# The first attention of a three-layer kernel: half of its modulation tiles moved into the output projection, its dense side work spread over two thirds of its units

## The chip, the cores and the metric

The kernel runs on one core of a Trainium2 chip. The core has TensorE (PE, matrix products into PSUM), VectorE (DVE), ScalarE (ACT), GpSimd (POOL) and SyncE (SP); here POOL and SP mostly start DMA transfers. Every engine runs its own instructions in order and waits for others on semaphores. The metric is the device time of one execution in microseconds; three runs were timed and one more was profiled.

## What is computed

The sequence has 512 rows of width 1024. A first block has two layers, a second block one. Each layer of the first block takes six vectors from a conditioning vector c, normalizes x, scales and shifts it, mixes, adds the result times a gate, and does the same with a feed-forward part. The change touches the first layer only, and in it these lines:

```python
cond = jax.nn.silu(c)
mod = cond @ ada_w[i] + ada_b[i]            # six vectors of 1024
sh1, sc1, g1, sh2, sc2, g2 = split(mod, 6)
h = rms_norm(x, norm_mix[i]) * (1.0 + sc1) + sh1
q, k, v = split(h @ w_in, 3)                # 16 heads of 64, q and k normalized
s = q k^T + bias                            # block-causal: the future is cut off
y = (softmax(s) v) @ w_out
x = x + g1 * y
h = rms_norm(x, norm_ffn[i]) * (1.0 + sc2) + sh2
x = x + g2 * (square(relu(h @ w1)) @ w2)
```

The gate g1 is needed when y is added, sc2 and sh2 when x is normalized right behind it, and g2 only at the end of the feed-forward part.

## The kernel before

**Dense products.** Weights come as 136 slabs of 128 x 2048. SP loads a slab into one of two `w_raw` buffers; ACT rounds it into `w_hi` (line 1022); DVE subtracts to get `w_lo` (line 1444, `split`). The activations are kept as such a pair too (`h_hi`, `h_lo`), and each product is three matmuls (`three`, line 472): high by high, high by low, low by high. Splits run one slab ahead of PE: slab n + 1 is split at the start of the step in which PE uses slab n. PSUM has eight banks; an engine that has emptied a bank says so in `acc_free`.

**Modulation tiles.** `mod` is not computed on PE. POOL loads one tile of 128 x 1024 of `ada_w` (512 KB) at a time (line 396) into one of two `ada_raw` buffers, and a single DVE instruction multiplies it with c and sums along the row (line 1472, `ada`); the result is one column of `mod`, 128 of its values. A tile's transfer is issued when the tile two before it has been used (`ada_used`). `ada_put` (line 1482) adds the offsets. In the first layer tiles 0 to 31 are used up to the end of the projections, tiles 32 to 39 are sc2, 40 to 47 are g2.

**The attention.** It is written out as steps s, one for each unit s of 64. A unit is one head and one block `it` of 128 query rows; with `it` from 0 to 3 the score width n grows from 128 to 512 columns, and eight units (four blocks of two heads) make a head pair. In step s:
- PE (`attention_a`, line 635 on) makes the scores of units s and s + 1 if s is even (line 643), the transposes of unit s - 4 (line 652), and for even s the products with v of units s - 6 and s - 5 (line 666), then calls `side`.
- DVE (line 1858 on) adds the bias and takes the row maximum of unit s (line 1869), splits a slab where the plan says so, and for odd s scales units s - 3 and s - 2 by the inverse row sums (lines 1878, 1880). Where s is 6 more than a multiple of 8 it takes the finished output of a head pair out of PSUM. At every fourth step from 8 to 68 it does one `ada` at the end of the step.
- ACT (line 1155 on) first does the slab's high part if the plan says so and copies a side unit's result (line 1145), then copies the transposes of unit s - 4 (line 1165) and takes the exponential of unit s (line 1171).

**The side work.** v of the last eight heads is not computed ahead. It is left as eight side units of 24 matmuls (`pair_a`: one block of rows times 256 columns) from two slabs, 10 and 11, four units each. The plan `SIDE_A` lists the steps at which PE does them; slab 11 is split at the first step listed, slab 12 at the fifth. `value_a` makes PE wait for all eight before head 8. Since the side units read `h_hi` and `h_lo`, into which the attention's outputs are to go, the outputs of the first three head pairs are kept in `a_oT` (`A_EARLY`), and turned into their high and low parts at the steps of `A_KEPT`.

**The output projection.** `tail` multiplies with slabs 12 to 15. PE takes slabs 12 and 13 whole (outputs 0 to 3 of eight), then slabs 14 and 15 for the first half of the columns, then both again for the second half. On DVE and ACT the order is: split slab 13, outputs 0 and 1, split slab 14, outputs 2 and 3, split slab 15, outputs 4 to 7 by halves. DVE adds an output to x (line 1523, halves line 1510), ACT squares it (line 1076), DVE accumulates the squares (line 1505); the sums are the next normalization's. `tail` takes a function that is called behind each of the first three splits; before the change none is given here.

Of the kernel before, what the change touches and what calls it, by code (L numbers as in the profile page):

```python
# [15 lines left out]
TT = T // P  # L16
# [29 lines left out]
ADA_TILES = 48  # L46
# [4 lines left out]
ADA_QKV = 16  # L51
# [2 lines left out]


A_HEADS, HD = 16, 64
A_EARLY = 3

SG_HALF, SG_GROUPS = 3072, 8

# [14 lines left out]
def program(nc, I, out, tab_d, tz_d):  # L75
    ctx = ExitStack()
    with ctx:
        sems = {}

        def sem(name):  # L80
            if name not in sems:
                sems[name] = ctx.enter_context(nc.semaphore(name))
            return sems[name]
# [64 lines left out]
        a_bias = at("a_bias", 48 * K, [P, 4, T])  # L148
# [170 lines left out]
        NUA, NUH = len(UNITS_A), len(UNITS_H)  # L319
# [15 lines left out]

                return s in self.starts[::self.uses]

        SIDE_A, SIDE_H = Side([4 * u for u in range(2 * TT)], TT), Side([1, 11, 22, 33, 44, 55], 2)
        A_KEPT = [32 + 2 * i for i in range(A_EARLY)]
        KCT_STEP = 4  # L340
        U_STEPS = {step: (n // 3, n % 3) for n, step in enumerate((15, 16, 17, 19, 20, 21, 24, 25, 26, 28, 29, 30))}
        CMP_STEPS = {step: (n // 3, n % 3) for n, step in enumerate((6, 9, 13, 23, 27, 31, 35, 38, 41, 46, 50, 57))}
# [42 lines left out]
        def _(gp):  # L385
# [5 lines left out]
            def ada(k0, k1):  # L391

                for k in range(k0, k1):
                    if k >= ADA_FIRST + 2:
                        gp.wait_ge(sem("ada_used"), k - 1)
                    gp.dma_start(ada_raw[:, k % 2, :], I["ada"][k]).then_inc(sem(f"ada_in{k % 2}"), 16)  # L396
# [1 line left out]
            ada(ADA_FIRST, 16 + ADA_QKV)  # L398

            gp.wait_ge(sem("acc_free"), 4 + 4 * len(A_WALK))  # L400
            for h in range(A_HEADS + 2):
                if h < A_HEADS:
                    if h >= 4:
                        gp.wait_ge(sem("s_done"), 2 * TT * (h // 2 - 1))
                    gp.dma_start(a_bias[:, h % 4, :], I["a_bias"][h]).then_inc(sem(f"bias_in{h % 4}"), 16)
                if h >= 2:
                    ada(16 + ADA_QKV + h - 2, 16 + ADA_QKV + h - 1)
            def s5_tables(layer):

                first = 48 if layer == 0 else 2 * ADA_TILES  # L410
                per, slots = ADA_FFN[layer]
                early = sum(x == 0 for x in slots)
                middle = early + sum(x == 1 for x in slots)
                for b in range(2):
                    blk, k = 2 * layer + b, first + 2 * b * per
                    if blk % 2:
                        gp.wait_ge(sem("tab_done"), blk)
                    gp.dma_start(s5_in[:], I["s5_in"][blk]).then_inc(sem("s5_in"), 16)
                    gp.dma_start(dsk[:], I["dsk"][blk]).then_inc(sem("s5_in"), 16)
                    ada(k + (2 if b else 0), k + per + early + 2)  # L420
                    gp.wait_ge(sem("ktp_done"), blk + 1)
                    for j in range(L):
                        gp.dma_start(tz_d[blk][CH * j:CH * (j + 1)], KTp[:, :, ZPAD - CH * j:ZPAD - CH * j + L * CH])\
                          .then_inc(sem("s5_stored"), 16)
                    ada(k + per + early + 2, k + per + middle + 2)
                    gp.wait_ge(sem("tab_done"), blk + 1)
                    gp.dma_start(tab_d[blk], s5_tab[:]).then_inc(sem("s5_stored"), 16)
                    ada(k + per + middle + 2, k + 2 * per + (0 if b else 2))
# [28 lines left out]
        def _(pe):  # L457
# [293 lines left out]
                return a_qT[r, h // 2, it * P:(it + 1) * P], a_kT[r, h // 2, 0:P * (it + 1)], P * (it + 1)  # L751

            def value_a(u, j):
                if u == (8, 0):
                    pe.wait_ge(sem("side_free"), 2 * TT)
                return a_v[:, j, u[0] * HD:(u[0] + 1) * HD]

            def pair_a(u, k, sl):
# [54 lines left out]
            for kind in range(2):  # L813
                pe.wait_ge(sem("bl_done"), kind + 1)
                b = bank()
                for half in range(2):
                    s = c.base("slab") % 2
# [62 lines left out]
            for s in range(NUH + 4):  # L880
                if s < NUH and s % 2 == 0:
                    i, it, br, _ = UNITS_H[s]
# [7 lines left out]
                u = s - 3  # L890
# [8 lines left out]
                u = s - 4  # L899
                if 0 <= u < NUH:  # L900
                    i, it, br, g = UNITS_H[u]
# [524 lines left out]
        def _(dve):  # L1426
# [51 lines left out]
            def ada_put():  # L1478

                n, first = c.base("ada") - ada_base[0], c("ada", ada_base[0] - c.base("ada"))  # L1480
                dve.wait_ge(sem("ada_used"), c("ada"))
                tt(mod[:, bass.ds(first, n)], mod_s[:, 0:n], mod_b[:, bass.ds(first, n)], ALU.add).then_inc(sem("mod_done"), 1)
                c.add("mod")
                dve.wait_ge(sem("mod_done"), c("mod"))
                ada_base[0] = c.base("ada")
# [374 lines left out]
            for s in range(8 * (KT - 1) + 15):  # L1860
                if s < NUA:
                    h, it = UNITS_A[s]
                    n = P * (it + 1)
                    if it == 0:
                        dve.wait_ge(sem(f"bias_in{h % 4}"), 16 * (h // 4 + 1))
                    dve.wait_ge(sem("s_full"), s // 2 + 1)
                    if s >= 6:
                        dve.wait_ge(sem("t_full"), s - 5)
                    V.tensor_tensor_reduce(out=a_p[:, s % 6, 0:n], in0=ps[s % 3][:, 0:n], in1=a_bias[:, h % 4, P * (TT - 1 - it):T], scale=-1.0,  # L1869
                                           scalar=3e38, op0=ALU.add, op1=ALU.min, accum_out=neg_max[:, s % 8:s % 8 + 1])\  # L1870
                     .then_inc(sem("s_done"), 1)
                if SIDE_A.slab(s):
                    split()
                u = s - 3
                if 0 <= u < NUA and s % 2:
                    n, h2 = P * (UNITS_A[u][1] + 1), slice(u % 8, u % 8 + 2)
                    dve.wait_ge(sem("e_done"), u + 2)
                    step(V.reciprocal(row_inv[:, h2], row_sum[:, h2]))
                    for v in (u, u + 1):
                        ts_(a_p[:, v % 6, 0:n], a_p[:, v % 6, 0:n], row_inv[:, v % 8:v % 8 + 1], None, ALU.mult).then_inc(sem("p_ready"), 1)  # L1880
                if s - 1 in A_KEPT:
                    i = A_KEPT.index(s - 1)
                    dve.wait_ge(sem("xo_hi"), i + 1)
                    tt(h_lo[:, i, :], a_oT[:, i, :], h_hi[:, i, :].bitcast(F32), ALU.subtract).then_inc(sem("xo_lo"), 1)
                i = (s - 14) // 8
                if s % 8 == 6 and 0 <= i < KT:
                    if i < A_EARLY:
                        dve.wait_ge(sem("o_full"), 4 * i + 4)
                        cp(a_oT[:, i, :], ps[5 + i % 2][:]).then_inc(sem("o_kept"), 1)
                    else:  # L1890
                        dve.wait_ge(sem("xo_hi"), i + 1)
                        tt(h_lo[:, i, :], ps[5 + i % 2][:], h_hi[:, i, :].bitcast(F32), ALU.subtract).then_inc(sem("xo_lo"), 1)
                q = (s - 8) // 4
                if s >= 8 and s % 4 == 0 and q < NUA // 4:
                    ada(1, 0)
                    if q % 8 == 7:
                        ada_put()
            c.add("slab", 2)
            c.add("full", 2 * (TT - 1))
            tail(16)  # L1900
            ffn(40, 0)


# [460 lines left out]
```

## Time and profile before

| what | us |
|---|---|
| median of three timed runs | 1863.2 |
| lowest and highest | 1859.7, 1863.59 |
| the profiled execution | 1858.95 |
| its span in the trace | 1857.1 |
| PE busy | 1767.8 (95%) |
| DVE busy | 1160.4 (62%) |
| ACT busy | 667.4 (36%) |

All of the trace's times count from the span's start. Matmuls are pipelined, so the length that a row gives to one is longer than the distance to the next; where it matters, starts are compared. "Idle before" is the time in which an engine waited ahead of an instruction, with what released it. The mean granted clock of TensorE over the run was 0.993 of full speed.

### The profile page before, as it was taken

The page shows a single profiled execution, that of the slowest core. Times are in us where ns is not written, and L with a number is a line of the kernel's source. Part 1 is how long each engine was busy: PE and PEld are TensorE (multiplying, and loading weights), DVE is VectorE, ACT ScalarE, POOL GpSimd, SP SyncE. Part 2 cuts the span into 40 slices and gives each one's busy share as a digit, 9 for nine tenths or more (in the row PEclk, how much of TensorE's full clock was granted, in tenths as well). Part 3 has the DMA queues.
Part 4 walks back from the last instruction along what each step waited for, and adds up shares of the span by engine and source line. Part 5 has one row for each costly group of instructions (what it writes and reads, how often), then busy time and mean ns, then how long its engine had stood idle before and what let it go on. Part 6 is the DMA issues. An engine that isn't in the chain of part 4 may idle for free.

```text
span 1857.1 us, 24326 instructions
## 1 busy us (share of the span) xinstructions
PE 1767.8 (95%) x9417; PEld 1473.6 (79%) x9417; DVE 1160.4 (62%) x2374; ACT 667.4 (36%) x1086; POOL 104.0 (6%) x198
## 2 busy tenths in 40 slices
PE   3998989999999999999999999999999999899999
PEld 3887748888888897887888888888888977777787
DVE  5777684877457656555545457875687479435574
ACT  2323573532232334233232235322323332365432
POOL 1001110001000100100000000010001100000000
PEclk9999999999999999999999999999999999999999
DMA  8444342334433515551323323445335322310351
GB/s 331 147 149 170 124 122 73 129 128 136 168 123 127 184 69 200 174 204 68 128 99 125 103 102 120 154 130 202 125 137 183 123 91 91 122 38 11 143 200 46
DMA packets 44911, 245.99 MB, mean 132 GB/s; under 512 B 6080, under 2 KB 6304, under 8 KB 26752
## 3 DMA queue, kind: packets, MB, share of 16 engines
q1 hardware_dynamic: 23712, 153.26, 23.1%
q0 software_dynamic: 21088, 91.21, 14.8%
q8 instruction: 75, 1.23, 0.3%
q14 instruction: 36, 0.29, 0.0%
HBM read 229.23 MB, written 15.22 MB: 132 GB/s over the span
## 4 chain that ended last, share of the span: by engine, by line
PE 81%; DVE 11%; ACT 3%; issue 2%; DMA 2%; SPq 0%; DVEq 0%; ACTq 0%
PE ps L472 70%; DVE w_lo L1444 2%; PE ps L907 2%; ACT w_hi L1022 1%; DVE ada_raw L1472 1%; DMA ada_raw<-in_ada 1%; PE ps L781 1%; PE ps L888 1%; PE ps L897 1%; DMA bv_g<-in_bv_g 1%; PE ps L652 1%; PE ps L643 1%; DVE a_p L1869 1%; PE ps L666 1%; DVE pre L1565 1%
## 5 line engine op out<-in xcount | busy, mean ns | idle before, releaser
L1444 DVE TENSOR_TENSOR w_lo<-w_raw,w_hi 128x2048 fp32r<-128x2048 f32 x136 | 311.7, 2292 | 152.0 <-ACT w_hi L1022 151.7
L1022 ACT ACTIVATE w_hi<-w_raw 128x2048 fp32r<-128x2048 f32 x136 | 259.9, 1912 | 368.9 <-PE ps L472 346.6
L472 PE MATMUL ps<-h_hi,w_hi 128*128 128x512 f32 (+1 forms) x1008 | 377.5, 375 | 7.0 <-DVE w_lo L1444 3.6
L472 PE MATMUL ps<-h_lo,w_hi 128*128 128x512 f32 (+1 forms) x1008 | 373.2, 370 | 0.0
L472 PE MATMUL ps<-h_hi,w_lo 128*128 128x512 f32 (+1 forms) x1008 | 372.9, 370 | 0.0
L472 PEld LDWEIGHTS ps<-h_hi,w_hi 128*128 128x128 f32 x1008 | 190.9, 189 | 40.1 <-issue 5.0
L472 PEld LDWEIGHTS ps<-h_hi,w_lo 128*128 128x128 f32 x1008 | 190.7, 189 | 32.3
L472 PEld LDWEIGHTS ps<-h_lo,w_hi 128*128 128x128 f32 x1008 | 191.0, 189 | 30.8
L472 PE MATMUL ps<-hid_hi,w_hi 128*128 128x512 f32 (+1 forms) x576 | 211.3, 367 | 0.0
L472 PE MATMUL ps<-hid_hi,w_lo 128*128 128x512 f32 (+1 forms) x576 | 210.6, 366 | 0.0
L472 PE MATMUL ps<-hid_lo,w_hi 128*128 128x512 f32 (+1 forms) x576 | 210.5, 366 | 0.0
L472 PE MATMUL ps<-w_hi,h_hi 128*128 128x512 f32 (+1 forms) x480 | 184.0, 383 | 6.8 <-DVE pre L1565 3.7
L472 PE MATMUL ps<-w_lo,h_hi 128*128 128x512 f32 (+1 forms) x480 | 181.8, 379 | 0.0
L472 PE MATMUL ps<-w_hi,h_lo 128*128 128x512 f32 (+1 forms) x480 | 181.7, 378 | 0.0
L1472 DVE CUSTOM_DVE_ANT_0 ada_raw<-ada_raw,cond 128x1024 f32<-128x1024 f32 x108 | 131.1, 1222 | 49.4 <-DMA ada_raw<-in_ada 48.3
L472 PEld LDWEIGHTS ps<-hid_hi,w_hi 128*128 128x128 f32 x576 | 108.6, 189 | 17.7
L472 PEld LDWEIGHTS ps<-hid_hi,w_lo 128*128 128x128 f32 x576 | 108.6, 189 | 17.5
L472 PEld LDWEIGHTS ps<-hid_lo,w_hi 128*128 128x128 f32 x576 | 108.6, 189 | 17.4
L396 POOL DMA_DIRECT2D ada_raw<-in_ada x108 | 58.3, 540 | 1064.8 <-DVE mod_s L1472 991.5
L472 PEld LDWEIGHTS ps<-w_hi,h_hi 128*128 128x128 f32 x480 | 91.8, 191 | 25.7 <-DVE pre L1565 4.0
L472 PEld LDWEIGHTS ps<-w_hi,h_lo 128*128 128x128 f32 x480 | 91.8, 191 | 16.6
L472 PEld LDWEIGHTS ps<-w_lo,h_hi 128*128 128x128 f32 x480 | 91.9, 191 | 16.0
(379 smaller groups left out, 2425.5 us busy)
## 6 DMA issues: line engine op xcount, KB each, us to landing
w_raw<-in_slabs SPq DMA_DIRECT2D x136, 1024.0 KB, 4.9
ada_raw<-in_ada POOLq DMA_DIRECT2D x108, 512.0 KB, 4.7
s_tables<-s_tab POOLq DMA_DIRECT2D x4, 2692.0 KB, 9.2
s_t<-s_tables POOLq DMA_DIRECT2D x4, 2692.0 KB, 9.7
ada_first<-in_ada SPq DMA_DIRECT2D x4, 1536.0 KB, 18.4
a_bias<-in_a_bias POOLq DMA_DIRECT2D x16, 256.0 KB, 3.6
xT<-in_xT SPq DMA_DIRECT2D x1, 2048.0 KB, 20.1
s_toeplitz<-KTp POOLq DMA_DIRECT2D x32, 64.0 KB, 3.3
```

The costliest lines, as they stand in the source:

```text
L396: gp.dma_start(ada_raw[:, k % 2, :], I["ada"][k]).then_inc(sem(f"ada_in{k % 2}"), 16)
L472: last = mm(o, l, r, start=start and n == 0, stop=stop and n == 2)
L643: last = mm(ps[(s + j) % 3][:, 0:n], q, k, start=True, stop=True)
L652: last = nc.tensor.transpose(ps[3 + u % 2][:, j:j + P], a_p[:, u % 6, j:j + P], ident[:])
L666: last = mm(ps[5 + i % 2][HD * par:HD * par + HD, it * P:(it + 1) * P], value(UNITS_A[u + par], j), a_pt[:, (u + par) % 4, j * P:(j + 1) * ...
L781: last = mm(b[:, t * P:(t + 1) * P], b_v[:, t, gm * P:(gm + 1) * P], b_ws[:, gm // 3, :], start=True, stop=True)
L888: last = mm(ps[(s + g) % 3][:, 0:n], hqr[r, i, ts], hk[r, br - 1, 0:n], start=True, stop=True)
L897: last = nc.tensor.transpose(ps[3 + u % 2][:, j:j + P], h_p[:, u % 5, j:j + P], ident[:])
L907: last = mm(o, h_pt[:, u % 3, j * P:(j + 1) * P], hv[:, j, vc], start=j == 0, stop=j == it)
L1022: A(w_hi[s][:], w_raw[:, s, :], ACT.Copy).then_inc(sem("hi_done"), 1)
L1444: tt(w_lo[s][:], w_raw[:, s, :], w_hi[s][:].bitcast(F32), ALU.subtract).then_inc(sem("lo_done"), 1)
L1472: V.tensor_tensor_reduce(out=w, in0=w, in1=cond[:, which, :], scale=1.0, scalar=0.0, op0=ALU.mult, op1=ALU.add, accum_out=mod_s[:, o:o + 1 ...
```

## The change

Three things are altered. The side units stand at steps 0, 8, 14, 20, 26, 30, 34 and 38 instead of 0, 4, ..., 28; with that the split of slab 12 moves from step 16 to step 26, PE waits for the first four units before head 8 and for all eight before head 12, four outputs are kept instead of three, and they are turned over at steps 41 to 44. The attention does eight `ada` (tiles 32 to 39, steps 8 to 36) instead of sixteen. The other eight (tiles 40 to 47) are done in the output projection: four behind the split of slab 13, four behind the split of slab 14, and `ada_put` behind the split of slab 15. POOL issues their transfers behind the last bias tiles instead of between them.

```diff
--- before.py
+++ after.py
@@ -54,7 +54,8 @@
 
 
 A_HEADS, HD = 16, 64
-A_EARLY = 3
+A_EARLY = 4
+A_ADA = 8
 
 SG_HALF, SG_GROUPS = 3072, 8
 
@@ -335,8 +336,8 @@
 
                 return s in self.starts[::self.uses]
 
-        SIDE_A, SIDE_H = Side([4 * u for u in range(2 * TT)], TT), Side([1, 11, 22, 33, 44, 55], 2)
-        A_KEPT = [32 + 2 * i for i in range(A_EARLY)]
+        SIDE_A, SIDE_H = Side([0, 8, 14, 20, 26, 30, 34, 38], TT), Side([1, 11, 22, 33, 44, 55], 2)
+        A_KEPT = [41 + i for i in range(A_EARLY)]
         KCT_STEP = 4
         U_STEPS = {step: (n // 3, n % 3) for n, step in enumerate((15, 16, 17, 19, 20, 21, 24, 25, 26, 28, 29, 30))}
         CMP_STEPS = {step: (n // 3, n % 3) for n, step in enumerate((6, 9, 13, 23, 27, 31, 35, 38, 41, 46, 50, 57))}
@@ -398,13 +399,14 @@
             ada(ADA_FIRST, 16 + ADA_QKV)
 
             gp.wait_ge(sem("acc_free"), 4 + 4 * len(A_WALK))
-            for h in range(A_HEADS + 2):
-                if h < A_HEADS:
-                    if h >= 4:
-                        gp.wait_ge(sem("s_done"), 2 * TT * (h // 2 - 1))
-                    gp.dma_start(a_bias[:, h % 4, :], I["a_bias"][h]).then_inc(sem(f"bias_in{h % 4}"), 16)
-                if h >= 2:
+            for h in range(A_HEADS):
+                if h >= 4:
+                    gp.wait_ge(sem("s_done"), 2 * TT * (h // 2 - 1))
+                gp.dma_start(a_bias[:, h % 4, :], I["a_bias"][h]).then_inc(sem(f"bias_in{h % 4}"), 16)
+                if 2 <= h < A_ADA + 2:
                     ada(16 + ADA_QKV + h - 2, 16 + ADA_QKV + h - 1)
+            ada(16 + ADA_QKV + A_ADA, ADA_TILES)
+
             def s5_tables(layer):
 
                 first = 48 if layer == 0 else 2 * ADA_TILES
@@ -751,8 +753,8 @@
                 return a_qT[r, h // 2, it * P:(it + 1) * P], a_kT[r, h // 2, 0:P * (it + 1)], P * (it + 1)
 
             def value_a(u, j):
-                if u == (8, 0):
-                    pe.wait_ge(sem("side_free"), 2 * TT)
+                if u in ((8, 0), (12, 0)):
+                    pe.wait_ge(sem("side_free"), TT if u[0] == 8 else 2 * TT)
                 return a_v[:, j, u[0] * HD:(u[0] + 1) * HD]
 
             def pair_a(u, k, sl):
@@ -1891,13 +1893,18 @@
                         dve.wait_ge(sem("xo_hi"), i + 1)
                         tt(h_lo[:, i, :], ps[5 + i % 2][:], h_hi[:, i, :].bitcast(F32), ALU.subtract).then_inc(sem("xo_lo"), 1)
                 q = (s - 8) // 4
-                if s >= 8 and s % 4 == 0 and q < NUA // 4:
+                if s >= 8 and s % 4 == 0 and q < A_ADA:
                     ada(1, 0)
-                    if q % 8 == 7:
+                    if q == A_ADA - 1:
                         ada_put()
             c.add("slab", 2)
             c.add("full", 2 * (TT - 1))
-            tail(16)
+            def last_tiles(s):
+                if s < 2:
+                    ada(4, 0)
+                else:
+                    ada_put()
+            tail(16, last_tiles)
             ffn(40, 0)
```

ACT's rows of the steps around the first split and the copies of side units (`a_v`), from the exponential of unit 14 to that of unit 17 or 16, before:

```order
L1171 ACTIVATE a_p,row_sum<-a_p,neg_max 128x512 [waits p_ready,s_done]
L1165 ACTIVATE a_pt<-ps 128x256 [waits o_full,t_full]
L1171 ACTIVATE a_p,row_sum<-a_p,neg_max 128x512 [waits p_ready,s_done]
L1022 ACTIVATE w_hi<-w_raw 128x2048 [waits slab_used,raw_in0]
L1165 ACTIVATE a_pt<-ps 128x384 [waits o_full,t_full]
L1171 ACTIVATE a_p,row_sum<-a_p,neg_max 128x128 [waits p_ready,s_done]
L1145 ACTIVATE a_v<-ps 128x256 [waits acc_full]
L1165 ACTIVATE a_pt<-ps 128x384 [waits o_full,t_full]
L1171 ACTIVATE a_p,row_sum<-a_p,neg_max 128x128 [waits p_ready,s_done]
```

and after:

```order
L1173 ACTIVATE a_p,row_sum<-a_p,neg_max 128x512 [waits p_ready,s_done]
L1147 ACTIVATE a_v<-ps 128x256 [waits acc_full]
L1167 ACTIVATE a_pt<-ps 128x256 [waits o_full,t_full]
L1173 ACTIVATE a_p,row_sum<-a_p,neg_max 128x512 [waits p_ready,s_done]
L1167 ACTIVATE a_pt<-ps 128x384 [waits o_full,t_full]
L1173 ACTIVATE a_p,row_sum<-a_p,neg_max 128x128 [waits p_ready,s_done]
L1167 ACTIVATE a_pt<-ps 128x384 [waits o_full,t_full]
L1173 ACTIVATE a_p,row_sum<-a_p,neg_max 128x128 [waits p_ready,s_done]
```

The copy that stood in step 17 (behind the side unit of step 16) is gone, one stands in step 15, and the high part of the next slab no longer stands ahead of the copy of unit 12's transposes (128x384).

DVE's rows from outputs 0 and 1 of the output projection (`xT<-ps`, 128x512) up to outputs 2 and 3, before:

```order
L1444 TENSOR_TENSOR w_lo_56<-w_raw,w_hi_54 128x2048 [waits hi_done]
L1523 SCALAR_TENSOR_TENSOR xT<-ps,mod,xT 128x512 [waits acc_full]
L1523 SCALAR_TENSOR_TENSOR xT<-ps,mod,xT 128x512 [waits slab_used]
L1444 TENSOR_TENSOR w_lo<-w_raw,w_hi 128x2048 [waits hi_done]
L1523 SCALAR_TENSOR_TENSOR xT<-ps,mod,xT 128x512 [waits acc_full]
L1505 TENSOR_TENSOR acc<-acc,sq_x 128x512 [waits nsq]
L1523 SCALAR_TENSOR_TENSOR xT<-ps,mod,xT 128x512 [waits slab_used]
L1505 TENSOR_TENSOR acc<-acc,sq_x 128x512 [waits nacc,nsq]
L1444 TENSOR_TENSOR w_lo_56<-w_raw,w_hi_54 128x2048 [waits hi_done]
```

and after, from the same two outputs to output 2:

```order
L1525 SCALAR_TENSOR_TENSOR xT<-ps,mod,xT 128x512 [waits acc_full]
L1525 SCALAR_TENSOR_TENSOR xT<-ps,mod,xT 128x512 [waits slab_used]
L1446 TENSOR_TENSOR w_lo<-w_raw,w_hi 128x2048 [waits hi_done]
L1474 ISA ada_raw,mod_s<-ada_raw,cond 128x1024 [waits ada_in0]
L1474 ISA mod_s 128x1
L1474 ISA ada_raw,mod_s<-ada_raw,cond 128x1024 [waits ada_in1]
L1474 ISA mod_s 128x1
L1474 ISA ada_raw,mod_s<-ada_raw,cond 128x1024 [waits ada_in0]
L1474 ISA mod_s 128x1
L1474 ISA ada_raw,mod_s<-ada_raw,cond 128x1024 [waits ada_in1]
L1474 ISA mod_s 128x1
L1525 SCALAR_TENSOR_TENSOR xT<-ps,mod,xT 128x512 [waits acc_full]
```

Between the split of slab 14 (`w_lo<-w_raw`) and output 2 there are now four tiles; four more stand in the same way between the split of slab 13 and output 0.

## Rows read from the trace of the kernel before

**Rows 1.** The page, part 1: busy us (share of the span) and instructions by engine.
```profile
PE 1767.8 (95%) x9417; PEld 1473.6 (79%) x9417; DVE 1160.4 (62%) x2374; ACT 667.4 (36%) x1086; POOL 104.0 (6%) x198
```

**Rows 2.** Stretches: start:end, length, busy us by engine, PEclk granted, DMA share, GB/s.
```profile
171.00:286.00 115.00, 101.84 (x800) 70.38 (x800) 81.40 (x272) 71.59 (x208) 18.67 (x32) 0.96 0.40 129
279.40:283.50 4.10, 4.10 (x30) 3.20 (x30) 3.61 (x9) 1.77 (x5) 0.00 (x0) 0.58 0.00 0
286.00:313.70 27.70, 27.70 (x146) 23.83 (x144) 11.72 (x11) 8.55 (x8) 0.00 (x0) 1.00 0.22 76
```

**Rows 3.** Waits of PE from 186 to 286: us in total, times, longest.
```profile
PE ps L652 <- DVE a_p L1880: 11.5, 17, 1.4
```

**Rows 4.** PE in time: start, us, operation, [idle before <- what ended it].
```profile
185.71 0.55 PE L652 MATMUL ps<-ident,a_p 128*128 128x128 f32 x3 [0.42 <-DVE a_p L1880]
...
201.77 0.55 PE L652 MATMUL ps<-ident,a_p 128*128 128x128 f32 x3 [1.02 <-DVE a_p L1880]
...
208.16 0.66 PE L652 MATMUL ps<-ident,a_p 128*128 128x128 f32 x4 [1.23 <-DVE a_p L1880]
...
243.80 0.44 PE L652 MATMUL ps<-ident,a_p 128*128 128x128 f32 x2 [0.61 <-DVE a_p L1880]
...
247.02 0.55 PE L652 MATMUL ps<-ident,a_p 128*128 128x128 f32 x3 [1.25 <-DVE a_p L1880]
...
249.51 0.66 PE L652 MATMUL ps<-ident,a_p 128*128 128x128 f32 x4 [0.25 <-DVE a_p L1880]
...
255.16 0.44 PE L652 MATMUL ps<-ident,a_p 128*128 128x128 f32 x2 [0.16 <-DVE a_p L1880]
...
279.32 0.55 PE L652 MATMUL ps<-ident,a_p 128*128 128x128 f32 x3 [1.45 <-DVE a_p L1880]
```

**Rows 5.** Stretches around one side unit: matmuls of line 472 and weight loads alone, PEclk.
```profile
171.20:177.30 6.10, 5.44 (x24) 5.19 (x24) 0.50 0.72 228
194.50:198.50 4.00, 3.14 (x24) 2.93 (x24) 1.00 0.35 104
```

**Rows 6.** DVE, ACT and PE in time, in the output projection.
```profile
288.56 2.29 DVE L1444 TENSOR_TENSOR w_lo<-w_raw,w_hi 128x2048 fp32r<-128x2048 f32 x1 [1.05 <-ACT w_hi L1022]
...
297.22 0.75 DVE L1523 SCALAR_TENSOR_TENSOR xT<-ps,mod,xT 128x512 f32<-128x512 f32 x1 [4.69 <-PE ps L472]
...
308.10 0.75 DVE L1523 SCALAR_TENSOR_TENSOR xT<-ps,mod,xT 128x512 f32<-128x512 f32 x1 [4.08 <-PE ps L472]
...
308.77 0.68 DVE L1505 TENSOR_TENSOR acc<-acc,sq_x 128x512 f32<-128x512 f32 x1
...
309.43 1.90 ACT L1022 ACTIVATE w_hi<-w_raw 128x2048 fp32r<-128x2048 f32 x1
...
311.36 2.29 DVE L1444 TENSOR_TENSOR w_lo<-w_raw,w_hi 128x2048 fp32r<-128x2048 f32 x1 [1.91 <-ACT w_hi L1022]
...
313.57 0.48 DVE L1510 SCALAR_TENSOR_TENSOR xT<-ps,mod,xT 128x256 f32<-128x256 f32 x1
...
313.70 0.39 PE L472 MATMUL ps<-h_hi,w_hi 128*128 128x256 f32 x1
```

**Rows 7.** DVE and POOL in time: four tiles in a row in the value panel.
```profile
154.62 1.22 DVE L1472 CUSTOM_DVE_ANT_0 ada_raw<-ada_raw,cond 128x1024 f32<-128x1024 f32 x1
...
156.14 0.53 POOL L396 DMA_DIRECT2D ada_raw<-in_ada  x1 [16.39 <-DVE mod_s L1472]
...
161.38 1.23 DVE L1472 CUSTOM_DVE_ANT_0 ada_raw<-ada_raw,cond 128x1024 f32<-128x1024 f32 x1 [4.39 <-DMA ada_raw<-in_ada]
...
163.76 2.29 DVE L1444 TENSOR_TENSOR w_lo<-w_raw,w_hi 128x2048 fp32r<-128x2048 f32 x1
```

**Rows 8.** Stretches around a stop of PE in the second layer.
```profile
837.40:841.50 4.10, 0.08 (x1) 0.00 (x0) 4.10 (x4) 0.60 (x1) 0.00 (x0) 0.76 0.00 0
841.50:845.50 4.00, 3.90 (x13) 3.52 (x14) 3.69 (x4) 0.15 (x1) 0.00 (x0) 0.50 0.14 20
```

**Rows 9.** POOL's issues of tiles at line 396, from 60 to 290.
```profile
DMA to landing us min/median/max: 3.6/4.0/6.8
```

## The prediction

> **What bounds the kernel now.** The page comes first: TensorE (PE) is busy 95% of the span and VectorE (DVE) 62% [rows 1], so time is lost or won only where PE waits, and the edits touch one stretch of about 160 us. The table by stretch shows it: the first attention runs from 171 to 286 us with PE busy 101.8 of 115 us at a mean granted clock of 0.96, while in its output projection (the `tail`, from 286) PE is busy for 27.7 us of 27.7 [rows 2]. The table of waits says who holds PE up in the attention: 17 waits on DVE's scaling of `a_p`, 11.5 us in all [rows 3].
>
> PE's order of time puts each at its unit step s [rows 4]. One of about 1.0 comes once per head pair, at s = 16, 24, 32, ...: after the widest scores (512 columns) DVE must reduce two units, move an output and scale, while PE has only narrow work left. Without the move (s = 8) it is 0.42. One of 0.25 (and a smaller one of 0.16) follows an `ada` beside which no dense side unit runs; 1.23 came at s = 18, where the slab's split is; 1.25 at s = 40, where the kept outputs are turned over; 1.45 at s = 64.
>
> **The change in the attention.** Sixteen `ada` of 1.22 us on DVE become eight, and the eight side units (24 matmuls, 3.1 us at full clock [rows 5]) go from s = 0, 4, ..., 28 to 0, 8, 14, 20, 26, 30, 34, 38. PE's own work stays. What changes is which wait has a side unit beside it:
> - s = 14, 30 and 38 put 3.1 us between the widest scores and the transposes that wait. The waits at s = 16, 32 (1.02 each) and 40 (1.25) go: -3.3.
> - The split at s = 16 moves to s = 26, behind a side unit and with no `ada` of its step. ACT's 1.9 and DVE's 2.3 then lie beside 3.1 of side unit and some 3 us of other PE work; the 1.23 falls back to the 0.25 of an uncovered `ada`: -1.0.
> - From s = 40 there is no `ada`: three waits of 0.25 and three of 0.16 go, -1.2. The once-a-pair wait of 1.0 stays: its chain holds no `ada`.
> - Against it: the `ada` at s = 12, 24 and 28 lose their cover, 0.16 + 0.25 + 0.16 = +0.6; without the unit at s = 4 DVE lies bare there, about +0.4 (one such wait without an `ada` is the 0.42); four kept outputs instead of three, packed into s = 42 to 45, add about a DVE copy's length at s = 46 to 48, +0.7; the wait of 0.61 at s = 38 shrinks by some 0.2, since no kept output lies before it.
> - At the end, s = 64 and 68 lose an `ada` each, but PE ran at a mean clock of 0.58 from 279.4 to 283.5, after waiting 1.45 [rows 2, 4], so its own work set the pace. If the clock now holds, (1 - 0.58) x 4.1 = 1.7 comes back, else nothing; I take 0.5, nearer the second, since the wait stays.
>
> The sum is -3.3 - 1.0 - 1.2 + 0.6 + 0.4 + 0.7 - 0.2 - 0.5 = -4.5. The bounds: nothing or a little worse (each wait that goes is replaced by the next one in DVE's chain), and 11.5, all that PE waits for the scaling.
>
> **The change in the output projection.** This is where I put the weight. Its program on each engine is in order. DVE splits slab 13, adds outputs 0 and 1 to x, splits slab 14, adds 2 and 3, splits slab 15. ACT squares an output after DVE added it and only then makes the high part of the next slab. The chain from adding an odd output to the next thing DVE does behind the low part is 308.10 -> 309.43 -> 311.36 -> 313.57, 5.47 us [rows 6]. PE takes slab 15 at 313.70: the second chain ends just before it is needed. There is no slack there: what DVE is late with output 3, PE waits.
>
> Now four `ada` stand behind the split of slab 13, ahead of output 0, and four behind the split of slab 14. Four in a row are in the trace, in the value panel: from the start at 154.62 to the end at 163.76 is 9.14 us, 4.6 of them work and 4.39 waiting for the third tile, whose transfer is issued only once the first has been used (two buffers) [rows 7]. Step by step, on the clock of the run before:
> - slab 13's low part starts at 288.56 and takes 2.21 to the next start, so it is done at 290.77; + 9.14 = 299.91. Output 0 and output 1 (ready at 297.22) are both late. Output 1 starts at 299.91 + 0.67 = 300.58; + 5.47: slab 14's low part is done at 306.05. PE wants it at about 308, so no wait yet.
> - + 9.14 = 315.19. Output 2 (0.67) and one accumulation (0.68) later, at 316.54 instead of 308.10, output 3 starts; + 5.47 = 322.0.
> - PE reaches slab 15 at 313.70 as before and waits until 322.0: **8.3 us**. The tiles before it have their banks.
>
> What stands behind the waiting matmul on PE is all that follows, and everything after is paced by PE, so the shift stays to the end; DVE's `ada_put` (0.3) lies beside the first half tile. Nor does POOL pay: its last eight transfers have only the next stage's behind them.
>
> **The clock.** A stop of that length costs more than itself. From 837.4 to 841.5 PE waits, and in the 4 us behind it the granted clock is 0.50, 1.2 GHz [rows 8]. The first side unit, after the stop ahead of the first scores, ran wholly at 0.50: 24 matmuls in 5.44 us against 3.14 at 1.00 [rows 5], 2.3 lost. Slab 15 follows with the same shapes, so I take **2.3**; [rows 8] alone give (1 - 0.50) x 4.0 = 2.0. The Trainium skill (TensorE: Matmul & The Clock Gate, Terms) prices a throttled stretch at its length times one minus the ratio granted. For the 5.44 us of the slow unit that would be 2.7, and the sum 0.4 higher; I keep the measured difference.
>
> **Sum.** -4.5 + 8.3 + 2.3 = +6.1 us. The profiled execution took 1858.95 (span 1857.1), so it would become 1865.1. The median of the three timed runs is 1863.2, 4.3 above; the same step on it gives 1869.3, and I forecast 1869.
>
> **Bounds of the tail's cost.** A tile of `ada` landed 3.6 to 6.8 us after its issue over the stretch, 4.0 in the middle [rows 9]; the four in a row correspond to 5.24 from 156.14 to 161.38 [rows 7]. Both groups of four run right after a slab's transfer was let go by the split, as in the value panel, so I take that. At 3.6 each group shortens by 1.64 and PE waits 5.0; at 6.8 it waits 11.4.
>
> **Rivals.**
> 1. *The tiles land promptly.* Half of all landed within 4.0. At 3.6 the sum is -4.5 + 5.0 + 2.3 = +2.8: 1866.0. Against it: behind a split the wait in the middle of a group was 4.39. The Trainium skill (DMA: Bandwidth & Descriptors, Anatomy of one DMA) gives about 2.0 us plus the bytes at 436 GB/s, which for 512 KB is 3.2 us and speaks for this rival; by it PE would wait about 4.2 and the sum would be +2.0. No row here shows a tile that fast. Chance 0.15.
> 2. *The attention gives next to nothing.* ACT's copy of a side unit stands ahead of its transposes' copy and exponential, so a side unit at s = 14 makes ACT wait for PE longer before the exponential that DVE's next scaling needs; the gain shrinks to 1. Sum -1 + 8.3 + 2.3 = +9.6: 1872.8. For it: in one step of the program after, that copy waits for the whole side unit. Against it: that exponential is needed two steps later. Chance 0.18.
> 3. *Faster: the cover works for every wait.* With eight `ada` less and a full clock the chain after the widest scores is never late, in covered pairs or in others, and the attention saves 11.5; with tiles landing at 3.6 the tail costs 5.0 + 2.3 = 7.3 and the sum is -4.2: 1859.0. It decides from the point where the attention saves more than the tail costs, 10.6 on my rows. Against it: the 1.0 per pair in the last three pairs stands in a chain that holds no `ada`, and no side unit is near. Chance 0.07.
> 4. *The stop is partly made good.* Behind slab 15's first tiles PE turns to sums that wait for ACT and DVE; if the slow clock only eats into such waits, the 2.3 is hidden and the sum is +3.8: 1867.0. Against it: the slow stretch falls on the tiles on which those waits hang. Chance 0.05.
>
> My forecast has 0.55. About 0.2% (3.7 us) is what a measurement of this kernel tells from no change. Slower by more than that: the forecast nearly whole, rival 2 and most of 4, 0.73. Within: most of rival 1, the rest of 4 and a run set that lies low, 0.19. Faster: rival 3 and a little, 0.08. The range from 1861 to 1875 reaches from an attention that saves 7 with prompt tiles (-7 + 5.0 + 2.3 = 0.3, less some 2 for a run set that lies low) to one that saves 2 with slow tiles (-2 + 11.4 + 2.3 = 11.7).
>
> **What would show it.** In the profile after, between the two attention ends: PE's waits on `a_p` sum to 7 or 8 instead of 11.5, none at s = 16, 32 and 40, still about 1.0 at s = 24, 56 and 64; the first matmul of the output projection starts 4 to 6 us earlier, near 281. In the tail: one wait of PE of 7 to 9 us for `w_lo`, in the middle of the half tiles, the granted clock at 0.5 behind it, and on DVE two stretches of four `ada` with one wait of 4 to 5 for the tile in each. If that wait of PE is missing or under 3, the forecast is wrong by its main term; if the projection starts at its old time, by its second.

## The result: slower by 0.4%, and the profile after

| eight timed runs each, us | before | changed |
|---|---|---|
| median | 1861.7 | 1867.95 |
| lowest and highest | 1859.2, 1863.72 | 1865.24, 1876.19 |
| ratio | | 1.0042, 95% interval 1.003 to 1.0054 |

The medians differ by 6.3 us; the forecast was a step of 6.1 and a time of 1869. The profiled execution is the longest of the eight: 1876.19, its span 1874.4. So its 17.3 us above the profile before must be split by place.

PE's waits between 165 and 350 us of the changed kernel (in total, times, longest), where [rows 3] stood before:

```profile
PE ps L474 <- DVE w_lo L1446: 10.2, 1, 10.2
PE ps L654 <- DVE a_p L1882: 6.7, 11, 1.4
```

The scaling's waits went from 17 with 11.5 us to 11 with 6.7. A single wait of 10.2 is new; it is called the stop below. PE in time, the attention's waits (they answer to [rows 4]) and the new one:

```profile
183.85 0.55 PE L654 MATMUL ps<-ident,a_p 128*128 128x128 f32 x3 [0.42 <-DVE a_p L1882]
...
201.56 0.66 PE L654 MATMUL ps<-ident,a_p 128*128 128x128 f32 x4 [0.28 <-DVE a_p L1882]
...
212.52 0.55 PE L654 MATMUL ps<-ident,a_p 128*128 128x128 f32 x3 [1.02 <-DVE a_p L1882]
...
239.45 0.44 PE L654 MATMUL ps<-ident,a_p 128*128 128x128 f32 x2 [0.48 <-DVE a_p L1882]
...
254.85 0.55 PE L654 MATMUL ps<-ident,a_p 128*128 128x128 f32 x3 [1.25 <-DVE a_p L1882]
...
266.60 0.55 PE L654 MATMUL ps<-ident,a_p 128*128 128x128 f32 x3 [1.02 <-DVE a_p L1882]
...
276.82 0.55 PE L654 MATMUL ps<-ident,a_p 128*128 128x128 f32 x3 [1.44 <-DVE a_p L1882]
...
282.19 0.50 PE L474 MATMUL ps<-h_hi,w_hi 128*128 128x512 f32 x1
...
320.19 0.58 PE L474 MATMUL ps<-h_hi,w_hi 128*128 128x256 f32 x1 [10.15 <-DVE w_lo L1446]
```

These are s = 8, 18, 24, 38, 48, 56 and 64: no row stands at s = 16, 32 or 40, and the 1.23 of s = 18 is down to 0.28. (The other four of the eleven, at s = 12, 26, 30 and 34, are 0.15, 0.24, 0.16 and 0.28.) The projection starts at 282.19; before it started at 286.00. DVE in time shows what PE waits for at 320.19 (it answers to [rows 6, 7]):

```profile
284.74 2.29 DVE L1446 TENSOR_TENSOR w_lo<-w_raw,w_hi 128x2048 fp32r<-128x2048 f32 x1 [1.11 <-ACT w_hi L1024]
286.95 1.22 DVE L1474 CUSTOM_DVE_ANT_0 ada_raw<-ada_raw,cond 128x1024 f32<-128x1024 f32 x1
...
295.42 1.23 DVE L1474 CUSTOM_DVE_ANT_0 ada_raw<-ada_raw,cond 128x1024 f32<-128x1024 f32 x1 [6.10 <-DMA ada_raw<-in_ada]
...
297.77 1.41 DVE L1525 SCALAR_TENSOR_TENSOR xT<-ps,mod,xT 128x512 f32<-128x512 f32 x2
301.68 2.29 DVE L1446 TENSOR_TENSOR w_lo<-w_raw,w_hi 128x2048 fp32r<-128x2048 f32 x1 [2.50 <-ACT w_hi L1024]
303.89 1.22 DVE L1474 CUSTOM_DVE_ANT_0 ada_raw<-ada_raw,cond 128x1024 f32<-128x1024 f32 x1
...
310.95 1.22 DVE L1474 CUSTOM_DVE_ANT_0 ada_raw<-ada_raw,cond 128x1024 f32<-128x1024 f32 x1 [4.70 <-DMA ada_raw<-in_ada]
...
314.60 0.75 DVE L1525 SCALAR_TENSOR_TENSOR xT<-ps,mod,xT 128x512 f32<-128x512 f32 x1
...
317.84 2.29 DVE L1446 TENSOR_TENSOR w_lo<-w_raw,w_hi 128x2048 fp32r<-128x2048 f32 x1 [1.90 <-ACT w_hi L1024]
```

Two groups of four tiles, each with one wait for its third. Outputs 0 and 1 are added in one go at 297.77, since both lay ready. From output 3 (314.60) the low part of slab 15 is complete 5.45 later, at 320.05, and PE goes on at 320.19.

The clock, by stretch: length, busy time by engine, the granted clock (third from the right), DMA:

```profile
255.40:260.00 4.60, 4.60 (x32) 2.95 (x32) 2.45 (x12) 2.83 (x9) 1.43 (x3) 0.63 0.78 257
279.40:282.20 2.80, 2.11 (x31) 1.53 (x27) 0.00 (x0) 0.70 (x2) 0.00 (x0) 1.00 0.00 0
320.00:330.00 10.00, 9.81 (x66) 9.81 (x67) 3.73 (x11) 3.16 (x6) 0.00 (x0) 0.78 0.29 107
1660.00:1680.00 20.00, 19.64 (x95) 16.68 (x95) 5.23 (x19) 10.31 (x27) 0.00 (x0) 0.50 0.00 1
```

At the attention's end the clock now holds (it was 0.58 in [rows 2]), but it falls at 255, behind the wait of s = 48. That wait does not explain the fall by itself: the second profile of this kernel (experiment 3) has the same 1.25 there and a granted clock of 1.00 from 255 to 260. The clock is 0.78 in the ten us behind the stop. The last row lies in the third layer's attention, which the change does not touch; there the clock was 1.00 before:

```profile
1660.00:1680.00 20.00, 17.73 (x116) 13.50 (x117) 9.28 (x28) 11.64 (x32) 0.00 (x0) 1.00 0.15 54
```

| the same event, us from the start | before | changed | apart |
|---|---|---|---|
| first scores of the attention | 171.13 | 172.03 | +0.9 |
| first matmul of the projection | 286.00 | 282.19 | -3.8 |
| PE takes slab 15 | 313.70 | 320.19 | +6.5 |
| first reciprocal of the next normalization | 323.72 | 332.03 | +8.3 |
| first scores of the third layer | 1614.1 | 1623.6 | +9.5 |
| last scores of the third layer | 1746.8 | 1764.1 | +17.3 |

The change's own stretches are over at +8.3. On the way to the third layer 1.2 more come on top. Some of that lies between 346 and 354, where the granted clock is 0.79 and was 1.00 before; experiments 1, 7, 8 and 9, which have no stop, have such a dip behind the same normalization too. About 8 of the 17.3 come from the half clock in the third layer (see the last experiment).

### The profile page after: what moved, and what is told of

It reads as the page before. It is cut to its first block, busy times and chain, and to the rows that moved or that the text cites. A ratio compares the mean times of both kernels' runs of the same rounds, so it can differ in the third digit from the quotient of the medians.

```text
span 1874.4 us, 24327 instructions
## 1 busy us (share of the span) xinstructions
PE 1782.5 (95%) x9417; PEld 1486.7 (79%) x9417; DVE 1161.3 (62%) x2375; ACT 667.6 (36%) x1086; POOL 103.5 (6%) x198
## 3 DMA queue, kind: packets, MB, share of 16 engines
q8 instruction: 75, 1.23, 0.3%
## 4 chain that ended last, share of the span: by engine, by line
PE 80%; DVE 12%; DMA 4%; ACT 3%; issue 2%; SPq 0%; DVEq 0%; ACTq 0%
PE ps L474 68%; DVE w_lo L1446 3%; DMA ada_raw<-in_ada 2%; PE ps L909 2%; DVE ada_raw L1474 2%; DMA ada_first<-in_ada 1%; PE ps L783 1%; PE ps L890 1%; ACT w_hi L1024 1%; PE ps L899 1%; PE ps L654 1%; PE ps L645 1%; PE ps L668 1%; DVE pre L1567 1%; PE ps L931 1%
```

## Experiments

The first four ran on one chip beside 35 runs of the kernel before (median 1861.63), the next four on another beside 32 (1861.1), the last on a third beside 9 (1860.55). "Attention" below is the time from its first scores to the projection's first matmul: 114.9 before, 110.2 in the changed kernel. The clock moves this length too: with the same waits for the scaling (6.7 us in 11) it was 110.2, 109.1, 107.8, 109.0 and 108.9 in five profiles (the changed kernel's two and experiments 4, 8 and 9). The longest of them is the one whose clock fell at 255; the other four have 1.00 from 255 to 260. So where two variants are compared by the attention, the sum of the waits is given as well.

### 1. The plan alone

```diff
 kernel before
-A_EARLY = 3
+A_EARLY = 4
-SIDE_A, ... Side([4 * u for u in range(2 * TT)], TT), ...
+SIDE_A, ... Side([0, 8, 14, 20, 26, 30, 34, 38], TT), ...
-A_KEPT = [32 + 2 * i for i in range(A_EARLY)]
+A_KEPT = [41 + i for i in range(A_EARLY)]
```

(with the new wait in `value_a`; all sixteen tiles stay in the attention)

> Only the side units, the kept outputs and the split of slab 12 move as in the change; all sixteen tiles stay in the attention and the output projection is as before. My theory: the waits at s = 16, 32 and 40 go, those of 0.25 and 0.16 behind the tiles of the second half stay, so the attention gains 2.5 to 4 us, no stop in the projection, ratio 0.998 to 0.999. Rival (the plan gives next to nothing): gain under 1 us, ratio 1.000. Rival (the loss lies elsewhere than in the moved tiles): slower than before by more than 0.2%.

Measured: 1859.32, ratio 0.9993 (0.9976 to 1.0009). PE waits for the scaling 9.2 us in 17 waits instead of 11.5, the attention is 113.1 (-1.8), and there is no wait for slab 15. The plan alone gives 1 to 2 us, less than the 2.5 to 4 expected and less than the interval can tell from nothing. The waits at s = 16, 32 and 40 are gone, as expected, but two wider ones came that the changed kernel does not have: 1.16 at s = 46 and 0.46 at s = 66. Between 255 and 260 the clock was 0.66 here as well.

### 2. The tiles alone

```diff
 changed kernel
-A_EARLY = 4
+A_EARLY = 3
-SIDE_A, ... Side([0, 8, 14, 20, 26, 30, 34, 38], TT), ...
+SIDE_A, ... Side([4 * u for u in range(2 * TT)], TT), ...
-A_KEPT = [41 + i for i in range(A_EARLY)]
+A_KEPT = [32 + 2 * i for i in range(A_EARLY)]
```

(with the old wait in `value_a`)

> Only the eight tiles move into the output projection; the side units stay at every fourth step. My theory: the attention gains 1 to 3 us from eight tiles fewer, PE stops 8 to 10 us ahead of slab 15 and then runs at half clock for about 5 us: +7 to +11 us, ratio 1.004 to 1.006, with one wait for w_lo of 8 to 10 us in its trace. Rival (the stop is not the cause): no more than 1.001.

Measured: 1867.6, ratio 1.0031 (1.0013 to 1.0049), 6.0 us, a little less than the 7 to 11 expected. The attention is 112.3 (-2.6), with waits of 10.3 us in 11. PE in time, at slab 15:

```profile
320.55 0.58 PE L474 MATMUL ps<-h_hi,w_hi 128*128 128x256 f32 x1 [9.45 <-DVE w_lo L1446]
```

So the loss comes with the tiles; the plan alone has none. In the attention the two parts' waits fall by 2.3 and 1.2, both together by 4.8: the changed kernel has 1.3 us more than the sum, about the wait of 1.16 that the plan alone brings. (The lengths, 1.8 and 2.6 against 4.7, seem to add up, but the clock has a share in each: all three have 1.00 at the end, where the kernel before had 0.58, and only two have the fall at 255.)

### 3. The changed kernel again

> The changed kernel once more. My theory: ratio 1.003 to 1.005; the stop ahead of slab 15 is again 8 to 10 us, while the stretch at half clock in the third layer, some 25 us long in the first profile, is an accident of that execution and is absent or elsewhere. Rival: it belongs to the change and stands at the same place again.

Measured: 1868.99, ratio 1.0043 (1.0025 to 1.0061). Stop 8.46, projection at 281.51, attention 109.1. The loss is the same, and the stop varies by 1.7 between two executions, with the tiles' landing: the third tiles waited 4.64 and 4.38 here against 6.10 and 4.70.

One half of the expectation failed. The stretch at half clock in the third layer was expected to be absent or elsewhere; it stands at nearly the same place again, from about 1654 to 1681, after 1656 to 1683 in the first profile. It is not what makes the loss, though: the lowest runs of the two kernels are 6.7 us apart here (1858.15 and 1864.88) and 6.0 in the first set (1859.2 and 1865.24), about as far as the medians. And the profile of experiment 2 has the stop, has a clock of 1.00 in the third layer from 1640 on, and still took 1867.85.

### 4. Eight tiles, spread over the projection

One tile behind the splits of slabs 13 and 14 each, and 2, 1, 2, 1 behind outputs 0 to 3:

```diff
 changed kernel
-                    ada(4, 0)
+                    ada((1, 1)[s], 0)
...
+                        between(o)      # in tail, behind output o: ada((2, 1, 2, 1)[o], 0)
```

> The change, but the eight tiles of the output projection are spread: one behind the split of slab 13, two behind output 0, one behind output 1, one behind the split of slab 14, two behind output 2, one behind output 3. DVE has gaps of 4.7, 2.5, 4.1 and 1.9 us there in the trace of before. My theory: PE's wait ahead of slab 15 is under 1.5 us and the clock stays full, the attention keeps its 4.7 us: 1856 to 1859 us, ratio 0.997 to 0.9985. Rival (the slower clock in the later layers makes the difference, not the stop): slower than before, as the change is, ratio about 1.004. Rival (the tiles' transfers decide wherever they stand): PE still waits 4 us or more.

Measured: 1862.8, ratio 1.0014 (0.9996 to 1.0033); PE's stop is down from 8.5 or more to 3.79, but it was expected to be under 1.5, and the time 1856 to 1859. It is close to the last rival's 4. DVE in time:

```profile
285.76 1.22 DVE L1474 CUSTOM_DVE_ANT_0 ada_raw<-ada_raw,cond 128x1024 f32<-128x1024 f32 x1
...
290.74 1.23 DVE L1474 CUSTOM_DVE_ANT_0 ada_raw<-ada_raw,cond 128x1024 f32<-128x1024 f32 x1 [3.76 <-DMA ada_raw<-in_ada]
...
304.04 1.23 DVE L1474 CUSTOM_DVE_ANT_0 ada_raw<-ada_raw,cond 128x1024 f32<-128x1024 f32 x1 [3.04 <-DMA ada_raw<-in_ada]
```

Counted from each split, the third tile still waits for its transfer, 3.76 us ahead of output 1 and 3.04 us ahead of output 3. Spreading the work does not do if the transfers are not in step.

### 5. One group, behind the split of slab 13

Tiles 40 to 43 go back into the attention (`A_ADA = 12`); of the other four:

```diff
 changed kernel
-                if s < 2:
+                if s == 0:
                     ada(4, 0)
+                elif s == 1:
+                    pass
                 else:
                     ada_put()
```

> The changed kernel with four tiles only in the output projection, all behind the split of slab 13; tiles 40 to 43 go back into the attention (steps 40 to 52). Theory (the chain of the prediction: the stop is output 3 being late, and ahead of output 1 there is slack for a group): DVE waits 4 to 6 us in the group, output 1 is added about 3 us late, slab 14's low part is ready near its old distance plus 3 from the projection's start, and PE does not wait for slab 15's low part at all. The attention gives 4.7 less 0.8 for the four tiles, so the time is about 3.9 below the kernel before: ratio 0.998. Rival (each group holds PE up by its own DVE work and transfer wait): a stop of about half of 8 to 10, so 4 to 5 us, and a ratio of 1.000 to 1.002.

Measured: 1859.81, ratio 0.9991 (0.9979 to 1.0003). Attention 112.0. DVE waits 4.68 for the third tile. What follows on DVE:

```profile
297.87 1.41 DVE L1525 SCALAR_TENSOR_TENSOR xT<-ps,mod,xT 128x512 f32<-128x512 f32 x2
301.77 2.29 DVE L1446 TENSOR_TENSOR w_lo<-w_raw,w_hi 128x2048 fp32r<-128x2048 f32 x1 [2.50 <-ACT w_hi L1024]
...
305.76 0.75 DVE L1525 SCALAR_TENSOR_TENSOR xT<-ps,mod,xT 128x512 f32<-128x512 f32 x1 [0.43 <-PE ps L474]
```

At output 3 DVE is waiting for PE again (0.43): the delay was swallowed whole. PE has no stop, as the theory said; the rival, by which each group costs a stop by itself, falls. The time fell short: 3.9 us below the kernel before were expected, 1.3 came, and the interval includes 1. In the profile the stretch from the first scores to the first reciprocal is 2.9 shorter than before, all of it in the attention. Why the medians show less is open; experiment 7, with the same waits in the attention and no stop either, is 1.9 lower.

### 6. One group, behind the split of slab 14

```diff
 changed kernel, A_ADA = 12
-                if s < 2:
+                if s == 0:
+                    pass
+                elif s == 1:
                     ada(4, 0)
                 else:
                     ada_put()
```

> As the run before, but the four tiles stand behind the split of slab 14. Theory: output 2 has to wait for 4.6 us of tiles and a transfer of 4 to 5 us, output 3 is added about 5 us late and PE stops for 4 to 6 us ahead of slab 15, with a half clock behind it (2.3). Sum -3.9 + 5 + 2.3 = +3.4: ratio 1.002. Against the run with the first group alone the difference is 7 us. Rival (each group costs by itself): both runs equal, 4 to 5 us of stop in each.

Measured: 1864.86, ratio 1.0024 (1.0015 to 1.0033). Attention 112.3, as in the run before. DVE in time, the third tile and output 3:

```profile
307.04 1.23 DVE L1474 CUSTOM_DVE_ANT_0 ada_raw<-ada_raw,cond 128x1024 f32<-128x1024 f32 x1 [4.49 <-DMA ada_raw<-in_ada]
...
310.68 0.74 DVE L1525 SCALAR_TENSOR_TENSOR xT<-ps,mod,xT 128x512 f32<-128x512 f32 x1
```

And PE in time, at slab 15:

```profile
316.27 0.58 PE L474 MATMUL ps<-h_hi,w_hi 128*128 128x256 f32 x1 [4.96 <-DVE w_lo L1446]
```

The same number of tiles, one split later, cost 4.96 us of PE. The two medians differ by 5.1 us (7 expected); from the first scores to the first reciprocal the two profiles differ by 7.9. Both groups together cost more than the sum, 8.5 to 10.2 against 0 and 5.0: the first uses up the slack, and then its delay is handed on to the second. The rows bear this out: the low part of slab 14 is complete 16.7 us after the projection's start here, and 21.7 and 20.3 after it in the changed kernel's two profiles. That is 5.0 and 3.6 later, and the stops are longer than this one by 5.2 and 3.5.

### 7. Four tiles in DVE's idle times

```diff
 changed kernel, A_ADA = 12
                 if s < 2:
-                    ada(4, 0)
+                    ada((0, 0)[s], 0)
...
+                        between(o)      # in tail, behind output o: ada((2, 0, 2, 0)[o], 0)
```

> As before, twelve tiles in the attention, but the four in the projection stand two between outputs 0 and 1 and two between outputs 2 and 3, where DVE was idle for 4.7 and 4.1 us, and none in a row waits for a transfer. Theory: DVE does not wait for a tile, PE has no stop, and the time is 3.9 below the kernel before: ratio 0.998. Rival (the tiles' transfers themselves hold up the slabs' loads, 2 MB beside them): the stop is still there, 2 us or more, wherever DVE uses them.

Measured: 1857.91, ratio 0.998 (0.997 to 0.9989). No wait of DVE for a tile, no stop of PE. As many tiles (2 MB) are loaded for the projection as in experiments 5 and 6, so the transfers hold nothing up by themselves. The profiled execution is the slowest of its eleven (1863.39): its attention took 115.4, longer than before, with two stretches at a granted clock of about 0.5 (from 255 and from 270 us), though its waits for the scaling are those of experiments 5 and 6, 8.3 us in 14.

### 8. All eight tiles in DVE's idle times

```diff
 changed kernel
                 if s < 2:
-                    ada(4, 0)
-                else:
+                    ada((1, 0)[s], 0)   # one behind the split of slab 13
+            def late_tiles(k):
+                ada((1, 2)[k], 0)
+                if k == 1:
                     ada_put()
...
+                        between(o)      # in tail, behind output o: ada((2, 0, 2, 0)[o], 0)
...
+                        late(0)         # behind scales()
+                late(1)                 # ahead of invert(0)
```

> The changed kernel with all eight tiles still in the projection, each in a place where DVE was idle and its transfer has had time: one behind the split of slab 13, two between outputs 0 and 1, two between outputs 2 and 3, one behind the scales and two ahead of the first reciprocal. Theory: DVE waits for at most one tile (2 us, inside the slack ahead of output 1), PE has no stop or one under 1 us, and the attention's 4.7 is kept: ratio 0.9975. Rival (eight tiles of DVE work, 9.8 us, are too much for the gaps, whose sum is about 14 with the transfers not in step): a stop of 2 to 4 us ahead of slab 15 as with the spread of eight tiles before, or ahead of the first normalized half; ratio 1.000 to 1.001.

Measured: 1856.43, ratio 0.998 (0.996 to 0.9999). DVE in time:

```profile
291.60 1.23 DVE L1474 CUSTOM_DVE_ANT_0 ada_raw<-ada_raw,cond 128x1024 f32<-128x1024 f32 x1 [4.28 <-DMA ada_raw<-in_ada]
...
301.76 0.74 DVE L1525 SCALAR_TENSOR_TENSOR xT<-ps,mod,xT 128x512 f32<-128x512 f32 x1
...
305.00 2.29 DVE L1446 TENSOR_TENSOR w_lo<-w_raw,w_hi 128x2048 fp32r<-128x2048 f32 x1 [1.90 <-ACT w_hi L1024]
...
317.43 0.17 DVE L1557 RECIPROCAL rstd<-stat 128x2 f32<-128x2 f32 x1 [0.73 <-ACT stat L1112]
```

One tile waits 4.28, more than the 2 us expected, but ahead of output 1, where it costs nothing. No wait of PE for `w_lo` is left; the waits for the scaling are the changed kernel's (6.7 in 11). The reciprocal comes at 317.43 against 323.72 before: -6.3.

### 9. The same kernel once more

> The kernel with all eight tiles in the gaps once more, for a narrower answer: the spread of one of its nine times (1868.0 beside eight at 1857.5 or less) left its interval at 0.996 to 0.9999. Theory (attention 4.7 shorter, no stop in the projection): ratio 0.9975, with an interval that excludes 1, and a profile with no wait of PE for the low part of slab 15. Rival (it only drew a good set of runs, and eight tiles of DVE work cost what the attention gives): ratio between 0.9985 and 1.0005.

Measured: 1853.7, ratio 0.9957 (0.9943 to 0.997), 6 runs against 9. Attention 108.9, no wait for slab 15. The interval excludes 1, as the theory had it. The gain is more than the 0.25% expected; the attention gave 5.9 in both profiles of this kernel and not 4.7. The waits are the same; the clock is not: it is 1.00 from 255 to 260 in both, where the changed kernel's first profile had 0.66 and lost 1.7. That is enough for the 1.2, though no run separates it. The gain by the median is larger still than those 5.9, and the rest is not accounted for. It is the fastest kernel of the study: it has the change's own plan and the same eight tiles in the projection, only at other places in DVE's order. Its profiled execution was the longest of its six (1863.14). It has no stop in the first layer, but it has the third layer's slow stretch, as its row by stretch shows:

```profile
1640.00:1665.00 25.00, 23.32 (x118) 19.75 (x118) 5.54 (x26) 14.80 (x35) 0.00 (x0) 0.55 0.00 1
```

Of the eleven profiles of this study four have that stretch, some 27 us long each time: the changed kernel's two, experiment 6's and this one. The kernel before does not have it in its one profile, but 5 of its 84 timed runs are at 1868.7 to 1871.0, where most lie at 1858 to 1863. Whether those have the stretch is not known, for none of them was profiled. This kernel has it, so it comes without the stop too. Whether the stop makes it more frequent is open: 5 of 12 runs of the changed kernel in experiment 3 were 1874 or more, 5 us and more above their median.

## Why the prediction was right

**The attention, -4.5: right, 4.7 measured.** The first matmul of the projection came 110.2 after the first scores instead of 114.9. The bullets held place by place: none at s = 16, 32, 40 (-3.3); 0.28 at s = 18 (-1.0); from s = 40 on only the once-a-pair waits; 0.15 and 0.16 where a tile lost its cover. "About +0.4" for the missing unit at s = 4 was 0.30, a wait for the row maximum ahead of the scores of 512 columns; the 0.54 ahead of those of 384 stood there before too. At s = 38 it was 0.48 instead of 0.4; a 0.28 at s = 34 was not foreseen. The kept outputs made 1.25 at s = 48, where 0.25 more than usual was paid and not 0.7. The waits together give 4.8 - 0.3 = 4.5. The clock's 0.5 was mis-sized: at the end 1.7 came back, and in the first profile it was lost again at 255 (1 - 0.63, times 4.6 = 1.7), so the net was about nothing. In the second profile it was not lost there, and the attention gave 5.8. That the sum of -4.5 met 4.7 so closely is in part luck, since the clock alone moves this length by 1 to 2 us from one execution to the next. Rival 2 (an attention that gives 1) falls with the rows. By experiments 1 and 2 neither part alone has the gain: their waits fall by 2.3 and 1.2, both together by 4.8.

**The stop, 8.3: the right place and chain, 10.15 and 8.46 measured.** Output 3 to the low part took 5.45 (5.47 before). What was short was the first group: 6.10 us for its third tile, where the pattern in the value panel had 4.39. That is 1.7 of the 1.85 that the profile has above the term; the second group's 4.70 gives 0.3, less small differences. The transfer of that tile took 6.95 from its issue at 288.47; the range had 6.8 as its upper end. Rival 1 (tiles landed within 3.6) falls: it needs a wait of 4.39 - 1.64 = 2.75 for a third tile, and in the eight groups of four of five profiles (the changed kernel's two, experiments 2, 5 and 6) the wait was 4.38 to 6.10. By the Trainium skill (DMA: Bandwidth & Descriptors, Anatomy of one DMA), whose fixed part and rate give an estimate of 3.2 us per tile, PE's stop would have been 4.2. The trace does not agree; the measurement decides, and in this stretch a tile takes 3.7 to 7.3.

"PE wants it at about 308, so no wait yet" was the claim that the first group alone costs nothing. Experiment 5 shows it by its rows (no wait of PE for a low part), experiment 6 shows that the second pays.

**The clock, 2.3: 1.8 to 2.6 measured.** From the split of slab 15 to the first reciprocal, which the kernel before, without a stop, passes in 12.36 (311.36 to 323.72), the changed kernel took 14.19 and 14.34 the second time, experiment 2 14.1, experiment 6 15.0. Experiments 5 and 7, without a stop, took 12.36 as well. Rival 4, by which this loss is hidden, falls. The Trainium skill (TensorE: Matmul & The Clock Gate, Terms) prices a slow stretch at its length times one minus the ratio: for the ten us at 0.78 that is an estimate of 2.2. The trace agrees roughly, with 1.8 lost. By medians experiment 6 shows none of it: it lies 5.1 above experiment 5, and the stop alone is 5.0.

**The sum.** In the first profile -4.7 + 10.15 + 1.8 = +7.3, and with the first scores 0.9 later that is the +8.3 of the reciprocal within 0.1. In the second the attention gave 5.8, with the same 6.7 us of waits: -5.8 + 8.46 + 2.0 = +4.7, and the first scores came 1.3 later, +6.0 in all. The step of the medians is 6.3 in the first set and 7.4 in the second. So the forecast held by its terms, with the stop 0 to 2 us too small. The shift stays to the end, as said: it was +8.3 at the reciprocal and +9.5 at the third layer, so nothing in between gave it back.

Rival 3, faster, failed as the change stands, but its point of decision (an attention that saves more than the tail costs) is met once the tail costs nothing: experiments 7 to 9.

## What to carry to other kernels

Before side work is put into a stage, write down for each engine where it is idle and what it is idle for: an idle time ahead of a result that comes late anyway is free, one behind a split whose successor is needed at once is not. Work that waits for a transfer brings the wait with it: with two buffers, two tiles in a row cost only their work where both had landed, and the third waited 4.4 to 6.1 us for its transfer in every group of four. And slack is spent once: a delay that costs nothing with one group is handed on when a second follows.

## What the runs showed of the hardware

- A 512 KB tile took 3.7 to 7.3 us from issue to landing between 165 and 350 us, and a median of 5.2 in the changed kernel's first profile against 3.9 before. In its projection the tiles issued at 288.47, 289.61, 305.40 and 306.55, each just behind the start of a slab's load, took 5.5 to 7.0; those issued at 296.95 and 298.14, with no such load near, took 3.7 and 4.8.
- TensorE ran at its lower level (0.50, 1.2 GHz) for some 27 us in the third layer in one profile of the kernel of experiments 8 and 9 and not in the other. The third layer's attention, first to last scores, took 140.4 to 140.5 us in three profiles with it and 131.0 to 132.8 in four without (before and experiments 1, 2 and 5). What sets it off was not found.
- The granted clock between 255 and 260 was 0.66 in one profile of the changed kernel and 1.00 in the other, with the same waits of PE ahead of it. So a single profile can mislead: the changed kernel's first stands 17.3 above the one before, of which the change's own stretches made 8.3.
